# Four fp32r passes for the scores, and values to tokens by block transposes and ScalarE transfers, in a hybrid encoder layer

## The chip, the cores and the metric

The kernel runs on one NeuronCore of one Trainium2 chip, in one launch. The time is the device time of that core in microseconds (us). TensorE (PE in the rows) multiplies, VectorE (DVE), ScalarE (ACT) and GpSimd (POOL) do elementwise work, SyncE (SP) and ScalarE issue the transfers (DMAs).

## The reference

One encoder layer over 512 tokens of 1024 channels, all in float32:

```python
x = x + 0.5 * swiglu(rmsnorm(x, ffn1_norm_g), ...)          # D_FF = 2816
h = rmsnorm(x, mix_norm_g)
aq, ak, av, hq, hff, hfb, hi, hg, ga, gb = split_columns(h @ w_in)
y_attn = axial_gqa_attention(aq, ak, av, q_norm_g, k_norm_g, cos, sin) @ w_branch_attn
y_hgrn = hgrn2_bidirectional(hq, hff, hfb, hi, hg, lb, hgrn_out_norm_g) @ w_branch_hgrn
x = x + (sigmoid(ga) * y_attn + sigmoid(gb) * y_hgrn) @ w_out
x = x + 0.5 * swiglu(rmsnorm(x, ffn2_norm_g), ...)
return rmsnorm(x, final_norm_g)
```

The attention has 8 query heads of 64 channels over 2 key heads. Each head of q and k is normalized (`rmsnorm`), rotated (`apply_rope`), and then `s = q k^T`, `p = softmax(s)`, `o = p v`. In the recurrence (`hgrn2_bidirectional`) `hi` is the value `v`, which is wanted with tokens on the partitions; `hq`, `hff`, `hfb` and `hg` are its query, its two forget gates and its output gate.

## The kernel before, in words

Five engines run programs of their own and meet at semaphores (`wait_ge`, `then_inc`). Each engine takes its instructions in program order, so an instruction that waits holds up all behind it on that engine. The order is written out by hand.

**Weights.** All big products have a "unit" of weights, a tile of 128 x 1024 float32 (512 KB). SyncE loads it into one of two `raw` slots. ScalarE copies it to `w_hi` as fp32r (`split_hi`, L422), VectorE writes the remainder `w_lo = raw - w_hi` (`split_lo`, L791). There are four slots of `w_hi` and `w_lo`, and splits run three units ahead (`AHEAD`). A slot has 1408 columns, of which the units of the projection use the first 1024. TensorE then runs 24 products per unit (8 tiles of 128 channels, each as w_hi*h_hi, w_hi*h_lo, w_lo*h_hi) into one PSUM bank of 128 x 512. With unit `i` finished, VectorE multiplies the bank by the token's norm factor `rs` and puts it into SBUF ("evacuation"; semaphore `proj_read`). Two banks alternate, so unit `i+2` waits for the evacuation of unit `i`.

**The projection.** `PROJ` lists its 26 units: av, ak, four aq, four hi, four hf, four hq, four hf, four hg. All engines loop over it (TensorE L1356, ScalarE L587, VectorE L1000, SyncE L280). Beside the units hang:
- For k and the four q tiles (m = 0 to 4): ScalarE squares, TensorE averages over a head (`head_mean`), ScalarE takes the bias copy, `Ln` and `Exp` at iterations 3 to 7, VectorE a Newton step (three instructions) and the product with the gain (`qn_done`), SyncE swaps halves by four transfers into `q_swap`, GpSimd multiplies by cos, and VectorE finishes the rotation at iterations 4 to 8 (`rope_done`).
- For the values (`V_TILES`: av at iteration 0, hi at iterations 6 to 9): after the evacuation into `v_tmp`, TensorE transposes four 128 x 128 blocks into a PSUM bank (L1371), and ScalarE copies them to `v_a` or `v_h` (L618).
- From iteration 9 (`FIRST_ITEM`) one attention item per unit, 16 in all, `q = i - 9`. After unit `i` TensorE computes the scores of item `q`, 128 queries by 512 keys, for two heads, as plain float32 products over 64 partitions (`scores`, L1321). They wait until ScalarE has taken the exponentials of item `q-1` (`p_done`). VectorE takes the row maxima, ScalarE the exponentials with their sums (`exp_scores`). At the next iteration VectorE inverts the sums, ScalarE normalizes (`normalize_probs`), and VectorE transposes the probabilities by 32 x 32 blocks (`prob_blocks`) ahead of the next maxima.
- SyncE copies `v_a` to `v_rep` by 32 small transfers, ahead of its loads at its iterations 13 to 16 (`V_SENDS`). SyncE's iteration `i` loads unit `i` once `w_lo` of unit `i-2` is written, so it stands some five iterations before VectorE's iteration `i`.

**Order in one ScalarE iteration** from item 0 on: `normalize_probs(q-1)`, `split_hi(i+3)`, the copy of values where there is one, `exp_scores(q)`. **Order in one VectorE iteration:** `inverse_sums(q-1)`, evacuation of unit `i`, `prob_blocks(q-1)` and the maxima of item `q` (`attention_step`), `split_lo(i+3)`.

Elsewhere ScalarE issues transfers as well: in the second FFN, `x_to_tokens` (L443) issues four per call, each of 32 partitions, between its activations.

## Time and profile before

| | us |
|---|---|
| median of 3 runs | 1132.91 |
| lowest, highest | 1132.46, 2531.6 |
| the profiled execution | 1132.66 |
| its span, first to last instruction | 1130.9 |
| TensorE busy, share of the span | 1122.2, 99% |
| VectorE busy | 628.8, 56% |
| ScalarE busy | 442.5, 39% |
| mean granted TensorE clock | 0.998 |

Busy time is that in which an instruction's record covers the engine. Matmul records overlap, since matmuls are pipelined: the record of one 128 x 512 product lasts 389 ns, but the next one starts some 227 ns later. So products are counted here by the distance of their starts. Instructions that issue a transfer are not counted as busy; ScalarE's stand in rows marked ACTq, SyncE's in rows marked SPq. The idle time behind them is put down to "issue".

### The profile page before, as it was taken

The page shows a single profiled execution, that of the slowest core. Times are in us where ns is not written, and L with a number is a line of the kernel's source. Part 1 is how long each engine was busy: PE and PEld are TensorE (multiplying, and loading weights), DVE is VectorE, ACT ScalarE, POOL GpSimd, SP SyncE. Part 2 cuts the span into 40 slices and gives each one's busy share as a digit, 9 for nine tenths or more (in the row PEclk, how much of TensorE's full clock was granted, in tenths as well). Part 3 has the DMA queues.
Part 4 walks back from the last instruction along what each step waited for, and adds up shares of the span by engine and source line. Part 5 has one row for each costly group of instructions (what it writes and reads, how often), then busy time and mean ns, then how long its engine had stood idle before and what let it go on. Part 6 is the DMA issues. An engine that isn't in the chain of part 4 may idle for free.

```text
span 1130.9 us, 16616 instructions
## 1 busy us (share of the span) xinstructions
PE 1122.2 (99%) x6359; PEld 908.6 (80%) x6359; DVE 628.8 (56%) x840; ACT 442.5 (39%) x658; POOL 81.5 (7%) x72
## 2 busy tenths in 40 slices
PE   9999999999999999999999999999999999999997
PEld 7888888888888777777788888888888888888886
DVE  6755555563332586647688767655555555542223
ACT  6423232232222444546856655534232323331223
POOL 0000000000000130000143320020000000000000
PEclk9999999999999999999999999999999999999999
DMA  6332322333322434212221222422244343332321
GB/s 198 124 111 75 111 92 93 108 113 103 103 95 74 172 110 133 75 57 75 76 79 57 74 76 93 168 93 93 79 126 121 91 120 108 119 110 93 99 88 75
DMA packets 51650, 114.78 MB, mean 101 GB/s; under 512 B 21904, under 2 KB 25104, under 8 KB 51344
## 3 DMA queue, kind: packets, MB, share of 16 engines
q1 hardware_dynamic: 32752, 105.16, 28.1%
q10 hardware_dynamic: 18848, 8.92, 2.7%
q8 instruction: 35, 0.57, 0.2%
q14 instruction: 15, 0.12, 0.0%
HBM read 105.41 MB, written 4.19 MB: 97 GB/s over the span
## 4 chain that ended last, share of the span: by engine, by line
PE 98%; DMA 1%; DVE 0%; ACT 0%; ACTq 0%; issue 0%; DVEq 0%
PE ps L1203 27%; PE ps L1205 27%; PE ps L1204 27%; PE ps L1229 4%; PE ps L1228 4%; PE ps L1230 4%; PE ps L1329 1%; PE ps L1346 1%; PE ps L1473 1%; DMA xT<-xT_dram 1%; PE ps L1466 0%; PE ps L1427 0%; PE ps L1449 0%; PE ps L1378 0%; PE ps L1416 0%; DMA raw<-up_dram 0%
## 5 line engine op out<-in xcount | busy, mean ns | idle before, releaser
L1203 PE MATMUL ps<-h_hi,w_hi 128*128 128x512 f32 x1024 | 407.3, 398 | 0.5 <-DVE w_lo L786 0.5
L1205 PE MATMUL ps<-h_hi,w_lo 128*128 128x512 f32 x1024 | 399.1, 390 | 0.0
L1204 PE MATMUL ps<-h_lo,w_hi 128*128 128x512 f32 x1024 | 398.8, 389 | 0.0
L786 DVE TENSOR_TENSOR w_lo<-raw,w_hi 128x1024 fp32r<-128x1024 f32 (+2 forms) x190 | 233.4, 1231 | 176.8 <-ACT w_hi L430 170.6
L430 ACT ACTIVATE w_hi<-raw 128x1024 fp32r<-128x1024 f32 (+1 forms) x182 | 194.7, 1080 | 182.8 <-PE ps L1205 74.3
L1203 PEld LDWEIGHTS ps<-h_hi,w_hi 128*128 128x128 f32 x1024 | 192.2, 188 | 55.8 <-issue 15.2
L1204 PEld LDWEIGHTS ps<-h_lo,w_hi 128*128 128x128 f32 x1024 | 192.3, 188 | 41.7 <-issue 2.9
L1205 PEld LDWEIGHTS ps<-h_hi,w_lo 128*128 128x128 f32 x1024 | 192.2, 188 | 40.6
L502 ACT ACTIVATE g_hi<-un 128x512 fp32r<-128x512 f32 (+1 forms) x44 | 27.8, 632 | 219.9 <-DVE un L786 219.9
L786 DVE TENSOR_TENSOR un<-ps,rs 128x512 f32<-128x512 f32 x44 | 30.4, 690 | 97.6 <-PE ps L1205 97.6
L1229 PE MATMUL ps<-w_hi,g_lo 128*128 128x512 f32 x176 | 68.5, 389 | 0.0
L1205 PE MATMUL ps<-g_hi,w_lo 128*128 128x512 f32 x176 | 68.5, 389 | 0.0
L1203 PE MATMUL ps<-g_hi,w_hi 128*128 128x512 f32 x176 | 68.5, 389 | 0.0
L1228 PE MATMUL ps<-w_hi,g_hi 128*128 128x512 f32 x176 | 68.5, 389 | 0.0
L1230 PE MATMUL ps<-w_lo,g_hi 128*128 128x512 f32 x176 | 68.5, 389 | 0.0
L1204 PE MATMUL ps<-g_lo,w_hi 128*128 128x512 f32 x176 | 68.5, 389 | 0.0
L786 DVE TENSOR_TENSOR g_lo<-un,g_hi 128x512 f32 (+1 forms) x44 | 30.5, 692 | 36.7 <-ACT g_hi L502 36.7
L438 ACT ACTIVATE sq<-xT 128x512 f32 (+1 forms) x16 | 10.1, 632 | 81.0 <-DVE xT L789 81.0
L558 ACT ACTIVATE prob<-ps,neg_max 128x512 f32<-128x512 f32 x32 | 21.7, 685 | 46.5 <-DVE neg_max L974 46.5
L1228 PEld LDWEIGHTS ps<-w_hi,g_hi 128*128 128x128 f32 x176 | 33.0, 188 | 6.9
L1205 PEld LDWEIGHTS ps<-g_hi,w_lo 128*128 128x128 f32 x176 | 33.0, 188 | 6.9
L1204 PEld LDWEIGHTS ps<-g_lo,w_hi 128*128 128x128 f32 x176 | 33.0, 188 | 6.9
(232 smaller groups left out, 1140.6 us busy)
## 6 DMA issues: line engine op xcount, KB each, us to landing
raw<-up_dram SPq DMA_DIRECT2D x86, 512.0 KB, 3.3
raw<-proj_dram SPq DMA_DIRECT2D x26, 512.0 KB, 3.3
raw<-down_dram SPq DMA_DIRECT2D x16, 704.0 KB, 4.0
raw<-down_dram SPq DMA_DIRECT2D x22, 512.0 KB, 3.3
raw<-gates_dram SPq DMA_DIRECT2D x16, 512.0 KB, 3.3
raw<-branch_dram SPq DMA_DIRECT2D x8, 512.0 KB, 3.3
raw<-wout_dram SPq DMA_DIRECT2D x8, 512.0 KB, 3.3
x_spill_dram<-xT ACTq DMA_DIRECT2D x1, 2048.0 KB, 7.1
```

Of the source, the lines that this page charges most:

```text
L430: A(w_hi[:, cst % 4, 0:width], raw[:, cst % 2, 0:width], ACT.Copy).then_inc(hi_done, 1)
L502: A(g_hi[:, 2 * it + q, :], un[:], ACT.Copy).then_inc(ghi_done, 1)
L558: A(prob[:, a, :], ps[:, 2 + a, :], ACT.Exp, bias=neg_max[:, q, a:a + 1], accum_out=prob_sum[:, q, a:a + 1]).then_inc(p_done, 1)
L786: return V.tensor_tensor(out, a, b, op)
L1203: T.matmul(ps[:, bank, :], w_hi[:, slot, cols], moving_hi(j), start=start and j == 0, stop=False)
L1204: T.matmul(ps[:, bank, :], w_hi[:, slot, cols], moving_lo(j), start=False, stop=False)
L1205: ins = T.matmul(ps[:, bank, :], w_lo[:, slot, cols], moving_hi(j), start=False, stop=stop and j == tiles - 1)
L1228: T.matmul(ps[:, bank, :], g_hi[:, j, rows], w_hi[:, slot, cols], start=first, stop=False)
L1229: T.matmul(ps[:, bank, :], g_lo[:, j, rows], w_hi[:, slot, cols], start=False, stop=False)
L1230: ins = T.matmul(ps[:, bank, :], g_hi[:, j, rows], w_lo[:, slot, cols], start=False, stop=end)
L1329: T.matmul(ps[:, 2 + a, :], qk[rows, 1 + t, P * qt:P * (qt + 1)], qk[rows, 0, :], start=True, stop=True).then_inc(s_done, 1)
L1346: ins = T.matmul(ps[rows, Y_BANK + i, GROUP * BLOCK * w:GROUP * BLOCK * (w + 1)], v_rep[j // 8][keys, j % 8, rows], probs.rearrange("p s c ...
```

## The change

**Scores.** The two float32 products of an item over 64 partitions become four fp32r products over 128 partitions. The keys are split into a high part, held twice (`k_twice`, both halves of the partitions), and a low part (`k_low`, also on both halves), in the free columns of the `w_hi` and `w_lo` slots. The queries of a head are split into `q_parts`: high part on one half of the partitions, low part on the other. ScalarE writes the high parts (`keys_twice` at iteration 6, four copies; `query_hi` at 7, 10, 13, 17, two copies each) and the second half of the low keys (`keys_low_swapped` at 9, two copies); VectorE writes the low parts (`keys_low` at 8, `query_low` at 8, 11, 14, 18, two instructions each).

**Splits ahead of norms.** At iterations 3 to 7 the splits of the weights stand ahead of the norm's instructions on both engines, and the Newton step's square moves from VectorE to ScalarE.

**Values to tokens.** hi moves behind the first four hf, to iterations 10 to 13. TensorE's transposes of hi and ScalarE's copies to `v_h` go. Instead VectorE transposes `v_tmp` in place by 32 x 32 blocks right after the evacuation, and ScalarE, after `exp_scores`, issues 16 transfers of 32 partitions x 4 x 32 elements (16 KB) that put the blocks in place in `v_h` (`values_to_tokens`). The next hi's evacuation on VectorE waits until all 16 have landed (`vh_loaded`), because they read `v_tmp`.

**Smaller things.** SyncE's first `v_rep` transfer also waits for `rope_done` 5. The sigmoids also wait for the last scores.

```diff
--- before.py
+++ after.py
@@ -61,11 +61,15 @@
 
 
 
-PROJ = ([("av", 0), ("ak", 0)] + [("aq", t) for t in range(4)] + [("hi", t) for t in range(4)]
-        + [("hf", h) for h in range(4)] + [("hq", t) for t in range(4)]
+PROJ = ([("av", 0), ("ak", 0)] + [("aq", t) for t in range(4)] + [("hf", h) for h in range(4)]
+        + [("hi", t) for t in range(4)] + [("hq", t) for t in range(4)]
         + [("hf", h) for h in range(4, HH)] + [("hg", t) for t in range(4)])
-V_TILES = {i: w for w, i in enumerate(i for i, (kind, _) in enumerate(PROJ) if kind in ("av", "hi"))}
+V_TILES = {0: 0}
+HI_AT = PROJ.index(("hi", 0))
 FIRST_ITEM = 9
+KEYS_AT = [6, 9]
+QUERY_AT = [7, FIRST_ITEM + 1, FIRST_ITEM + 4, FIRST_ITEM + 8]
+LOW_AT = [8, FIRST_ITEM + 2, FIRST_ITEM + 5, FIRST_ITEM + 9]
 BLOCK = 32
 BLOCKS = S // BLOCK
 QUADS = P // BLOCK
@@ -169,8 +173,13 @@
         q_cos = prob
         q_swap = [at("q_swap0", 16, [P, S]), at("q_swap1", 18, [P, S])]
         v_tmp = at("v_tmp", 85, [P, S])
+        q_parts = [at("q_parts0", 32, [P, 2, S], F32R)] + [at(f"q_parts{n}", kib, [P, 2, S], F32R) for n, kib in ((1, 87), (2, 91))]
+        q_parts.append(q_parts[1])
+        k_twice = [w_hi[:, 2 * a:2 * a + 2, UW:UW + S // 2] for a in range(2)]
+        k_low = [w_lo[:, 2 * a:2 * a + 2, UW:UW + S // 2] for a in range(2)]
         q_sq, q_ms, q_rs, q_t = (at(n, 87 + 2 * i, [P, S]) for i, n in enumerate(("q_sq", "q_ms", "q_rs", "q_t")))
         silu_tmp = [q_sq, q_ms, q_rs, q_t]
+        q_t = [q_t, at("q_t1", 82, [P, S])]
 
         k_in = [at("k_in0", 64, [P, S]), sq_sum]
         b_cum = [at("b_cum0", 66, [P, S]), at("b_cum1", 68, [P, S])]
...
@@ -290,6 +302,7 @@
                             to = i - V_SENDS
                             if to == 0:
                                 sp.wait_ge(vn_done, 1)
+                                sp.wait_ge(rope_done, 5)
                             for half in range(2):
                                 for quad in range(QUADS):
                                     sp.dma_start(v_rep[half][BLOCK * to:BLOCK * (to + 1), quad::QUADS, :],
@@ -550,6 +563,38 @@
                     split_hi(2)
             ffn(1)
 
+            halves = lambda k: k.rearrange("p (s c) -> p s c", s=2)
+
+            def keys_twice():
+                act.wait_ge(rope_done, 1)
+                for a, rows in enumerate(head_rows):
+                    for to in (rows, head_rows[1 - a]):
+                        A(k_twice[a][to], halves(qk[rows, 0, :]), ACT.Copy).then_inc(khi_done, 1)
+
+            def keys_low_swapped():
+                act.wait_ge(klo_done, 2)
+                for a, rows in enumerate(head_rows):
+                    A(k_low[a][head_rows[1 - a]], k_low[a][rows].bitcast(F32), ACT.Copy).then_inc(kls_done, 1)
+
+            def query_hi(t):
+                act.wait_ge(rope_done, t + 2)
+                if t == 0:
+                    act.wait_ge(qsq_done, 1)
+                elif t < 3:
+                    act.wait_ge(rope_done, 5)
+                else:
+                    act.wait_ge(s_done, 16)
+                for a, rows in enumerate(head_rows):
+                    A(q_parts[t][rows, a, :], qk[rows, 1 + t, :], ACT.Copy).then_inc(qhi_done, 1)
+
+            def values_to_tokens(w):
+                act.wait_ge(vblk_done, w + 1)
+                blocks = v_tmp[:].rearrange("p (t j c) -> p t j c", j=QUADS, c=BLOCK)
+                for quad in range(QUADS):
+                    for to in range(QUADS):
+                        act.dma_start(v_h[BLOCK * to:BLOCK * (to + 1), :, P * w + BLOCK * quad:P * w + BLOCK * (quad + 1)],
+                                      blocks[BLOCK * quad:BLOCK * (quad + 1), :, to, :]).then_inc(vh_loaded, 16)
+
             def exp_scores(q):
                 for a in range(2):
                     act.wait_ge(nm_done, 2 * q + 1 + a)
@@ -571,6 +616,7 @@
             def sigmoids():
 
                 act.wait_ge(proj_read, len(PROJ) + BANK_CREDIT)
+                act.wait_ge(s_done, 2 * ITEMS)
                 for j in range(HH):
                     A(forget[:, j, :], forget[:, j, :], ACT.Sigmoid).then_inc(fs_done, 1)
                     if j >= 4:
@@ -590,6 +636,7 @@
                     act.wait_ge(lb_ready, 1)
                     A(lbt[:], lbt[:], ACT.Exp).then_inc(lb_exp, 1)
                 if 3 <= i <= 7:
+                    split_hi(base + i + AHEAD)
                     m = i - 3
                     act.wait_ge(qms_done, m + 1)
                     if m:
@@ -599,9 +646,17 @@
                     A(q_rs[:], q_ms[:], ACT.Ln).then_inc(act_seq, 1)
                     act.wait_ge(act_seq, m + 1)
                     A(q_rs[:], q_rs[:], ACT.Exp, scale=-0.5).then_inc(qr_done, 1)
+                    act.wait_ge(qr_done, m + 1)
+                    if m >= 2:
+                        act.wait_ge(rope_done, m - 1)
+                    A(q_t[m % 2][:], q_rs[:], ACT.Square).then_inc(qy_done, 1)
+                if i in KEYS_AT:
+                    (keys_twice, keys_low_swapped)[KEYS_AT.index(i)]()
+                if i in QUERY_AT:
+                    query_hi(QUERY_AT.index(i))
                 if 0 <= i - FIRST_ITEM - 1 < ITEMS:
                     normalize_probs(i - FIRST_ITEM - 1)
-                for n in {0: (0, 1), 1: ()}.get(i, (i,)):
+                for n in {0: (0, 1), 1: ()}.get(i, () if 3 <= i <= 7 else (i,)):
                     split_hi(base + n + AHEAD)
                 if i == 0:
                     rms_estimate(1)
@@ -615,13 +670,15 @@
                 if w is not None:
                     act.wait_ge(vt_done, w + 1)
                     vt = ps[:, 7, :].rearrange("p (a b) -> p a b", b=P)
-                    A(v_a[:] if w == 0 else v_h[:, :, P * (w - 1):P * w], vt, ACT.Copy).then_inc(vn_done, 1)
+                    A(v_a[:], vt, ACT.Copy).then_inc(vn_done, 1)
                 q = i - FIRST_ITEM
                 if q == Y_AT:
                     y_hi(0)
                     y_hi(1)
                 if 0 <= q < ITEMS:
                     exp_scores(q)
+                if kind == "hi":
+                    values_to_tokens(t)
             gate_base = BASE["gates"]
 
 
@@ -947,6 +1004,19 @@
                 tt(by_quad(ya_lo[:, t, :]), ps[:, Y_BANK:Y_BANK + QUADS, P * t:P * (t + 1)].rearrange("p i (s c) -> p s i c", c=BLOCK),
                    by_quad(ya_hi[:, t, :].bitcast(F32)), ALU.subtract).then_inc(yalo_done, 1)
 
+            halves = lambda k: k.rearrange("p (s c) -> p s c", s=2)
+
+            def keys_low():
+                dve.wait_ge(khi_done, 4)
+                for a, rows in enumerate(head_rows):
+                    tt(k_low[a][rows], halves(qk[rows, 0, :]), k_twice[a][rows].bitcast(F32), ALU.subtract).then_inc(klo_done, 1)
+
+            def query_low(t):
+                dve.wait_ge(qhi_done, 2 * t + 2)
+                for a, rows in enumerate(head_rows):
+                    tt(q_parts[t][head_rows[1 - a], a, :], qk[rows, 1 + t, :], q_parts[t][rows, a, :].bitcast(F32),
+                       ALU.subtract).then_inc(qlo_done, 1)
+
             def inverse_sums(q):
                 dve.wait_ge(p_done, 2 * q + 2)
                 V.reciprocal(inv_sum[:, q, :], prob_sum[:, q, :]).then_inc(inv_done, 1)
@@ -1001,15 +1071,17 @@
                 if i == 2:
                     lower_bound()
                 if 3 <= i <= 7:
+                    split_lo(base + i + AHEAD)
                     m = i - 3
-                    dve.wait_ge(qr_done, m + 1)
-                    link(newton(q_rs[:], q_ms[:], q_t[:]))
+                    dve.wait_ge(qy_done, m + 1)
+                    link(stt(q_t[m % 2][:], q_t[m % 2][:], -0.5, q_ms[:], ALU.mult, ALU.mult))
+                    link(stt(q_rs[:], q_t[m % 2][:], 1.5, q_rs[:], ALU.add, ALU.mult))
                     stt(qk[:, m, :], qk[:, m, :], gain[:, 33:34] if m == 0 else gq8[:], q_rs[:],
                         ALU.mult, ALU.mult).then_inc(qn_done, 1)
                     dve.wait_ge(qn_done, m + 1)
                 if 0 <= i - FIRST_ITEM - 1 < ITEMS:
                     inverse_sums(i - FIRST_ITEM - 1)
-                if i != 1 and i < FIRST_ITEM:
+                if i != 1 and i < FIRST_ITEM and not 3 <= i <= 7:
                     split_lo(base + i + AHEAD)
                 if i == 0:
                     split_lo(base + 1 + AHEAD)
@@ -1017,24 +1089,32 @@
                 if i - FIRST_ITEM == Y_AT:
                     y_lo(0)
                     y_lo(1)
-                w = V_TILES.get(i)
-                if w:
-                    dve.wait_ge(vt_done, w)
+                if kind == "hi":
+                    dve.wait_ge(*((vh_loaded, 16 * QUADS * QUADS * t) if t else (vt_done, 1)))
                 dst = {"av": v_tmp[:], "hi": v_tmp[:], "ak": qk[:, 0, :], "aq": qk[:, min(1 + t, 4), :], "hf": forget[:, t, :],
                        "hq": hq[:, t % 4, :], "hg": hgate[:, t % 4, :]}[kind]
                 dve.wait_ge(unit_done, base + i + 1 + W_CREDIT)
                 tt(dst, ps[:, i % 2, :], rs[:], ALU.mult).then_inc(proj_read, 1)
+                if i == LOW_AT[0]:
+                    keys_low()
                 if 4 <= i <= 8:
                     m = i - 4
                     dve.wait_ge(mix_loaded, 16)
                     dve.wait_ge(qswap_done[m % 2], 64 * (m // 2 + 1))
-                    link(tt(q_t[:], q_swap[m % 2][:], c["sin"], ALU.mult))
+                    link(tt(q_t[m % 2][:], q_swap[m % 2][:], c["sin"], ALU.mult))
                     dve.wait_ge(cos_done, m + 1)
-                    tt(qk[:, m, :], q_cos[:, m % 2, :], q_t[:], ALU.add).then_inc(rope_done, 1)
+                    tt(qk[:, m, :], q_cos[:, m % 2, :], q_t[m % 2][:], ALU.add).then_inc(rope_done, 1)
                     dve.wait_ge(rope_done, m + 1)
+                if i == LOW_AT[0]:
+                    query_low(0)
+                if kind == "hi":
+                    dve.wait_ge(proj_read, i + 1 + BANK_CREDIT)
+                    V.transpose(v_tmp[:], v_tmp[:]).then_inc(vblk_done, 1)
                 attention_step(i - FIRST_ITEM)
                 if i >= FIRST_ITEM:
                     split_lo(base + i + AHEAD)
+                if i in LOW_AT[1:]:
+                    query_low(LOW_AT.index(i))
             gate_base = BASE["gates"]
 
             def gate_lo(g):
@@ -1321,19 +1401,22 @@
             def scores(q):
                 t, qt = q // 4, q % 4
                 if q == 0:
-                    pe.wait_ge(rope_done, 5)
+                    pe.wait_ge(khi_done, 4)
+                    pe.wait_ge(kls_done, 2)
+                if qt == 0:
+                    pe.wait_ge(qlo_done, 2 * t + 2)
                 for a in range(2):
                     if q:
                         pe.wait_ge(p_done, 2 * q - 1 + a)
-                    rows = slice(HD * a, HD * (a + 1))
-                    T.matmul(ps[:, 2 + a, :], qk[rows, 1 + t, P * qt:P * (qt + 1)], qk[rows, 0, :],
-                             start=True, stop=True).then_inc(s_done, 1)
+                    queries = q_parts[t][:, a, P * qt:P * (qt + 1)]
+                    T.matmul(ps[:, 2 + a, :], queries, k_twice[a], start=True, stop=False)
+                    T.matmul(ps[:, 2 + a, :], queries, k_low[a], start=False, stop=True).then_inc(s_done, 1)
 
             def weighted(w):
                 if w == 0:
                     pe.wait_ge(vrep_loaded, 16 * 2 * QUADS * QUADS)
                     pe.wait_ge(qeps_done, 5)
-                    pe.wait_ge(vn_done, 5)
+                    pe.wait_ge(vn_done, 1)
                 else:
                     pe.wait_ge(yalo_done, 2 * w)
                 pe.wait_ge(pt_done, TURNS * GROUP * (w + 1))
@@ -1439,7 +1522,7 @@
             def contributions(u):
                 pe.wait_ge(kn_done, u + 1)
                 if u == 0:
-                    pe.wait_ge(vn_done, 5)
+                    pe.wait_ge(vh_loaded, 16 * QUADS * QUADS * 4)
                 if u >= 3:
                     pe.wait_ge(oeps_done, (u - 1) // 2)
                 for n in range(NSUP):
```

## Rows read from the trace of the kernel before

**Rows 1.** The page: busy time of each engine, and the chain that ended last by engine.
```profile
PE 1122.2 (99%) x6359; PEld 908.6 (80%) x6359; DVE 628.8 (56%) x840; ACT 442.5 (39%) x658; POOL 81.5 (7%) x72
PE 98%; DMA 1%; DVE 0%; ACT 0%; ACTq 0%; issue 0%; DVEq 0%
```

**Rows 2.** TensorE's longest wait in the whole span: us in total, times, longest.
```profile
PE ps L1315 <- POOL g_lo L316: 1.3, 1, 1.3
```

**Rows 3.** The chain in order of time: start us, us, what (L1371 transposes, L1329 scores).
```profile
417.71 0.44 PE ps L1371 x4
...
423.64 0.44 PE ps L1371 x4
...
443.97 1.06 PE ps L1329 x4
...
450.71 1.06 PE ps L1329 x4
...
851.90 0.23 PE ps L1204
...
862.78 0.23 PE ps L1204
```

**Rows 4.** ScalarE in order of time, second FFN: start, length, what, idle before it.
```profile
823.94 2.59 ACTq L448 DMA_DIRECT2D x_tok<-xT  x4
826.63 2.01 ACT L430 ACTIVATE w_hi<-raw 128x1024 fp32r<-128x1024 f32 x2 [2.07 <-issue]
```

**Rows 5.** Busy us by stretch, before item 0: PE, PEld, DVE, ACT, POOL, PEclk, DMA, GB/s.
```profile
372.00:430.00 58.00, 57.90 (x253) 45.34 (x251) 42.66 (x60) 26.40 (x38) 11.61 (x5) 1.00 0.41 139
```

**Rows 6.** VectorE in order of time, iteration 10 (item 1).
```profile
436.80 0.69 DVE L786 TENSOR_TENSOR forget<-ps,rs 128x512 f32<-128x512 f32 x1 [3.20 <-PE ps L1205]
437.41 0.70 DVE L962 STREAM_TRANSPOSE prob_t<-prob 128x512 f32<-128x512 f32 x1
438.04 0.85 DVE L965 STREAM_TRANSPOSE prob_t<-prob 128x128 f32<-128x128 f32 x4
438.81 1.25 DVE L974 TENSOR_REDUCE neg_max<-ps 128x1 f32<-128x512 f32 x2
```

**Rows 7.** SyncE in order of time, and VectorE's last rotation, before item 0.
```profile
424.15 6.71 SPq L295 DMA_DIRECT2D v_rep<-v_a  x8
...
427.66 0.69 DVE L786 TENSOR_TENSOR qk<-prob,q_t 128x512 f32<-128x512 f32 x1
```

**Rows 8.** Instructions that issue transfers, by tile: ns min/median/max; below, time to landing.
```profile
L448 ACTq DMA_DIRECT2D x_tok<-xT x64: 592/632/744, 815.0 to 976.2; - x64
...
L295 SPq DMA_DIRECT2D v_rep<-v_a x32: 585/597/1778, 424.2 to 447.5; - x32
...
L298 SPq DMA_DIRECT2D raw<-proj_dram x26: 327/328/586, 333.7 to 516.2; - x26
...
DMA to landing us min/median/max: 1.8/1.9/3.9
```

**Rows 9.** ScalarE in order of time, item 1.
```profile
439.49 0.69 ACT L558 ACTIVATE prob<-ps,neg_max 128x512 f32<-128x512 f32 x1 [1.66 <-DVE neg_max L974]
...
440.74 0.20 ACT L558 ACTIVATION_READ_ACCUMULATOR prob<-ps,neg_max 128x1 f32 x1
441.30 1.34 ACT L564 ACTIVATE prob<-prob,inv_sum 128x512 f32<-128x512 f32 x2 [0.36 <-DVE inv_sum L952]
```

**Rows 10.** The end of the span, by stretches: TensorE busy first, PEclk after POOL.
```profile
1124.00:1126.00 2.00, 0.35 (x2) 0.00 (x0) 1.66 (x5) 1.57 (x4) 0.00 (x0) 1.00 0.38 145
1126.00:1128.00 2.00, 0.00 (x0) 0.00 (x0) 1.21 (x4) 1.09 (x3) 0.00 (x0) 0.67 0.59 228
1128.00:1130.90 2.90, 0.00 (x0) 0.00 (x0) 0.00 (x0) 0.00 (x0) 0.00 (x0) 0.50 0.47 181
```

**Rows 11.** TensorE in order of time, the start of the span.
```profile
1.32 5.06 PE L1315 MATMUL ps<-g_lo 128*128 128x512 f32 x11 [1.32 <-POOL g_lo L316]
...
8.41 0.61 PE L1263 MATMUL ps<-h_hi,w_hi 128*128 128x512 f32 x2
```

More of the change, by code:

```diff
@@ L215, in build @@
         vt_done, vn_done = sem("vt_done"), sem("vn_done")
+        vblk_done, vh_loaded = sem("vblk_done"), sem("vh_loaded")
         qsq_done, qms_done, qeps_done, qr_done = sem("qsq_done"), sem("qms_done"), sem("qeps_done"), sem("qr_done")
-        cos_done = sem("cos_done")
+        cos_done, qy_done = sem("cos_done"), sem("qy_done")
+        khi_done, klo_done, kls_done = sem("khi_done"), sem("klo_done"), sem("kls_done")
+        qhi_done, qlo_done = sem("qhi_done"), sem("qlo_done")
         qn_done, rope_done = sem("qn_done"), sem("rope_done")
```

## The prediction

> **What bounds the kernel now.** I read the page first: TensorE is busy for 99% of the span and the chain of waits that ended last runs on it for 98% [rows 1]. Then TensorE's waits: the longest is 1.3 us, at the very start [rows 2]. So in this kernel every TensorE product taken away is time saved, and every wait of TensorE that appears is time lost; nothing else counts. Then the chain in order of time, for what one step costs TensorE. A unit with nothing beside it takes (862.78 - 851.90) / 2 = 5.44 us (48 products, two units), a unit with a transpose of values 423.64 - 417.71 = 5.93, a unit with a score item 450.71 - 443.97 = 6.74 [rows 3]. Last I read what ScalarE pays for issuing a transfer, because the change gives it 64 more: four take 2.59 us, and the split behind them begins only when they are through, with 2.07 us of idle time put down to "issue" [rows 4]. ScalarE does not work while it issues.
>
> **What the change takes from TensorE.** Scores: an item costs 6.74 - 5.44 = 1.30 us now. Four fp32r products of 128 x 512 at the pace of a unit's (5.44 / 24 = 0.227 us) are 0.91. Saved: 16 x 0.39 = 6.2 us. No row has products with these operands; the bounds are 0.91 (same engine, same size, same kind) and 1.30 (nothing gained), and I take the first, since the new products have the form of a unit's. Transposes: 4 x (5.93 - 5.44) = 2.0 us. Together **8.2 us less**, if nothing waits.
>
> **The stretch before item 0.** At iterations 3 to 7 VectorE loses a square of 0.7 us per round and ScalarE gains it, which is busy for 26.4 of the 58 us of this stretch [rows 5]; the new copies of keys and queries (eight of some 0.6 us before item 0) fit beside it. The tight place is VectorE at iteration 8. With TensorE's transposes gone, unit 8 ends at 417.7 + 5.44 = 423.1 (start of the first removed transpose plus a unit) and unit 9 at 428.6. From 423.1 on VectorE does evacuation, `keys_low` (2), the two instructions of the rotation and `query_low` (2), seven instructions of 0.6 to 0.7 us [rows 6]: done at about 427.8. Item 0 is then ready 0.8 us before TensorE wants it. I cost this at nothing, bounds 0 and 2 us. The rotation ends near 426.5, where it ended at 428.3 before, but SyncE now holds the first eight `v_rep` transfers until then, where they began at 424.15 [rows 7]; they take 6.7 us at most, so raw 13, behind them on that queue, is issued near 433 and has landed by 437 (3.9 at most [rows 8]), so that ScalarE can split it ahead of item 1's exponentials at 438. Nothing, again because of cover: the loss is 0 to 2 us if that cover is gone.
>
> **The four hi iterations.** Here I see the loss. ScalarE issues 16 transfers behind the exponentials of each of items 1 to 4. At 2.59 / 4 = 0.645 us each [rows 4] that is **10.3 us in which ScalarE stands still**, in an iteration that TensorE wants to do in 5.44 + 0.91 = 6.35. Behind them on ScalarE wait the next normalization, the next split and the next exponentials, and TensorE's scores of item q wait for the exponentials of item q-1. Besides, VectorE waits for the landing before it evacuates the next hi, and behind that evacuation stand the block transposes and the maxima which those same exponentials need. One turn of this ring, from end of exponentials to end of exponentials:
> - 15 issues of 0.645, then 1.9 from the last issue to landing [rows 8]: 11.6 us; 0.1 for the signal.
> - VectorE: evacuation 0.61 (start to start), the new transpose 0.63 and a wait of 0.1 for the write before it, `prob_blocks` 438.81 - 437.41 = 1.40 [rows 6]; then from first maximum to first exponential 0.68 and the exponentials 440.94 - 439.49 = 1.45 [rows 6, 9]. Sum 4.9.
>
> A turn is 16.6 us against 6.35. The fourth train delays no evacuation, since iteration 14 is hq; there the ring is 10.3 of issue, then 1.34 of normalization, 0.8 for the last block transposes, and 0.68 + 1.45: 14.6 us.
>
> Now the clock times. Unit 9 ends at 428.6, unit 10 at 428.6 + 6.35 = 434.95, and the exponentials of item 1 end at 434.95 + 4.9 = 439.8. The next three ends are 456.4, 473.0, 489.6, and after the fourth train 504.2. The first head's exponential, which releases TensorE, is 0.65 earlier each time. TensorE wants item 2's scores at 441.3 (nothing to wait for) and item 3's at 447.65:
> - item 3: 455.8 instead of 447.65, waits 8.1 us
> - items 4 and 5: each a turn later, less unit and scores (5.44 + 1.1, since the second head now waits for its own exponential): 16.6 - 6.5 = 10.1 us each
> - item 6: 14.6 - 6.5 = 8.1 us
>
> With the 0.2 us per item that makes **37.1 us**. After item 6 ScalarE has no train any more and the ring (about 6.3 us) fits into the unit again. What is late next: nothing, the splits of units 16 and 17 are written inside the last two waits.
>
> **The clock.** The waits of 8 to 10 us are long enough to lose TensorE's clock. The last product of this kernel ends at 1124.35; the granted clock is 1.00 up to 1126, 0.67 in the next two microseconds and 0.50 after [rows 10]: it fell from 2.4 to 1.2 GHz between 2 and 3 us after the work stopped. What a return costs is seen at the start: 11 products take 5.06 us, 0.46 each, twice 0.227, and at 8.41 two take 0.61 together, the full pace [rows 11]. So some 6 us of work go at half pace, a loss of 3 us. Inside the ring this is free (unit and scores of 6.5 us become 9.5, the turn is 16.6); only after the fourth wait is it on the path. I take **3 us**; bounds 0 and 3.
>
> The Trainium skill, page "TensorE: Matmul & The Clock Gate", section "HAM oscillation — how this bites in real kernels", says that a kernel which waits between groups of products falls back to the lower level and pays the return at each such wait. By that rule there would be four returns to pay; the end of this trace agrees on the fall, no row shows how often the return is paid.
>
> **Sum.** 1132.66 (the profiled execution; 0.25 below the median, the span is 1130.9) - 8.2 + 37.1 + 3.0 = **1164.6, say 1165 us**, 2.8% slower.
>
> **Rivals.**
> - *Issuing is cheap.* SyncE's loads of 128 partitions take 0.33 us to issue, not 0.6 [rows 8]. If the new transfers did, with 128 pieces each instead of x_tok's 256: a turn is 11.9 us, the waits 3.4, 5.3, 5.3 and 3.6, with the 0.2s about 18; 1132.7 - 8.2 + 18 + 1 = 1143. Against it: `v_rep`, with 32 partitions and only 64 pieces, takes 0.597 [rows 8], so the number of pieces is not what costs. Chance 0.13.
> - *Issuing is hidden altogether* (not slower): the instructions only pass into a queue and ScalarE goes on, the landing of 2 us fits into the unit, and only TensorE's saving is left: 1132.66 - 8.2 = 1124.5. It holds if ScalarE's next activation begins within about 2 us of a train's start. Against it the idle time of 2.07 us behind four issues [rows 4]. Chance 0.07.
> - *Trains cost more.* No row has 16 issues in a row from ScalarE. The slowest x_tok issue took 0.744, landing took up to 3.9 and one `v_rep` issue 1.78 where loads stood on the same queue [rows 8]. In the first train SyncE issues `v_rep` at the same time. At 0.744 and with 3.9 to land three times: 37 + 6.3 + 6 = 49 us, 1177. Chance 0.12.
> - *Each return is paid.* If unit and scores at half pace came to stand in the ring after all (the second head's scores wait inside it), four returns of 3 us cost 12 instead of 3: 1174. Against it: a turn leaves 7 us after such a unit. The Trainium skill's section on HAM oscillation is on this side. Chance 0.02.
> - *The passes save nothing*, or item 0 stalls: 2 to 6 us on top of the forecast, 1167 to 1171. Chance 0.05, on top of any of the others; within the range.
>
> The Trainium skill, page "DMA: Bandwidth & Descriptors", section "Issuing engines are not separate DMA queues", says that the sequencer's time to start a transfer is usually small against the transfer. By it the second rival would hold and the time be 1124.5; here four issues occupy 2.59 us and one transfer lands in 1.9, so the trace disagrees, and the rival gets 0.07.
>
> **How the numbers follow.** Forecast 0.66 (1155 to 1172: issues of 0.585 to 0.70, the clock's 0 to 3 us), dearer trains 0.12 (to 1180), four returns 0.02, cheap issues 0.13 (1143, up to 1155), hidden 0.07 (1124). The range 1145 to 1180 leaves out the last, half of the cheap case and a little above: under 2 in 10. What a measurement can tell from no change is about 2%, here 23 us, so 1156 upward is slower: the forecast but for its lowest edge, the dear case and the four returns, 0.78. Within 2%: 0.21. Faster by 2% would need 22.7 us off TensorE, and 8.2 is all that is taken away: 0.01.
>
> **What would show it.** In the changed kernel's TensorE waits, four that end with ScalarE's exponentials, of about 8, 10, 10 and 8 us, between 447 and 504, and nothing of size elsewhere. In ScalarE's order of time, four trains of 16 issues, 10 us each, with no activation inside. On VectorE three waits for landings of about 10 us. The granted clock at 0.5 in part of that stretch. Score items outside it with 6.35 us from unit to unit. I am wrong if activations begin during a train, if the issues take 0.33, or if TensorE's gap per item stays at 6.74.

## The result, and the profile after

| | before | changed |
|---|---|---|
| median, us | 1132.92 (4 runs) | 1164.14 (4 runs, 1163.08 to 1164.68) |
| span of the profiled execution | 1130.9 | 1161.3 |
| mean granted clock | 0.998 | 0.986 |

The ratio is 1.0277, 95% interval 1.0263 to 1.0291: **slower by 2.8%**, 31.2 us. The forecast was 1165. (One run of the kernel before took 2531.6 us; the comparison leaves it out.)

The page of the changed kernel, against [rows 1]: TensorE's busy time hardly moves and its share falls, so most of the added time is time without work (the idle time grows from 8.7 to 36.9 us). The chain now runs for 3% of the span through ScalarE's issuing instructions.

```profile
PE 1124.4 (97%) x6343; PEld 920.4 (79%) x6343; DVE 635.9 (55%) x849; ACT 451.7 (39%) x673; POOL 76.4 (7%) x72
PE 87%; DVE 5%; ACTq 3%; ACT 2%; DMA 1%; issue 1%; DVEq 0%
```

TensorE's waits in the changed kernel (total, times, longest), against [rows 2]: five for the exponentials (L603; four are of size, the fifth is 0.6 us at item 11), the one at the very start, and one for the low part of the queries.

```profile
PE ps L1412 <- ACT prob L603: 27.6, 5, 7.4
PE ps L1395 <- POOL g_lo L329: 1.3, 1, 1.3
PE ps L1412 <- DVE q_parts L843: 0.7, 1, 0.7
```

TensorE in order of time in the changed kernel, the first of an item's four passes, items 2 to 8:

```profile
441.86 0.39 PE L1412 MATMUL ps<-w_hi,q_parts 128*128 128x512 f32 x1
...
455.81 0.80 PE L1412 MATMUL ps<-w_hi,q_parts 128*128 128x512 f32 x1 [7.44 <-ACT prob L603]
...
471.54 0.77 PE L1412 MATMUL ps<-w_hi,q_parts 128*128 128x512 f32 x1 [6.89 <-ACT prob L603]
...
487.90 0.80 PE L1412 MATMUL ps<-w_hi,q_parts 128*128 128x512 f32 x1 [6.96 <-ACT prob L603]
...
501.80 0.79 PE L1412 MATMUL ps<-w_hi,q_parts 128*128 128x512 f32 x1 [5.70 <-ACT prob L603]
...
509.71 0.39 PE L1412 MATMUL ps<-w_hi,q_parts 128*128 128x512 f32 x1
...
516.05 0.39 PE L1412 MATMUL ps<-w_hi,q_parts 128*128 128x512 f32 x1
```

Where nothing disturbs, an item and its unit take 516.05 - 509.71 = 6.34 us, where they took 6.74 [rows 3]. The four intervals before are 13.95, 15.73, 16.36 and 13.90 long, together 34.6 us more than 4 x 6.34. The idle times in brackets add up to 27.0 only, because after each wait the products ran at half pace (0.43 from start to start instead of 0.23) and filled a part of the next interval. Read the loss from starts, not from idle times.

ScalarE in order of time in the changed kernel, around the second train, items 2 and 3:

```profile
454.98 0.69 ACT L603 ACTIVATE prob<-ps,neg_max 128x512 f32<-128x512 f32 x1 [2.34 <-DVE neg_max L1044]
455.56 0.19 ACT L603 ACTIVATION_READ_ACCUMULATOR prob<-ps,neg_max 128x1 f32 x1
455.58 0.59 ACTq L595 DMA_DIRECT2D v_h<-v_tmp  x1
455.66 0.68 ACT L603 ACTIVATE prob<-ps,neg_max 128x512 f32<-128x512 f32 x1
456.21 0.62 ACTq L595 DMA_DIRECT2D v_h<-v_tmp  x1
456.23 0.20 ACT L603 ACTIVATION_READ_ACCUMULATOR prob<-ps,neg_max 128x1 f32 x1
456.86 9.10 ACTq L595 DMA_DIRECT2D v_h<-v_tmp  x14
466.01 1.33 ACT L609 ACTIVATE prob<-prob,inv_sum 128x512 f32<-128x512 f32 x2 [9.58 <-issue]
467.25 1.04 ACT L443 ACTIVATE w_hi<-raw 128x1024 fp32r<-128x1024 f32 x1
470.62 0.69 ACT L603 ACTIVATE prob<-ps,neg_max 128x512 f32<-128x512 f32 x1 [2.33 <-DVE neg_max L1044]
```

The train is there, 10.4 us for 16 issues (0.65 each), and nothing behind it begins before it is over. Its first two issues, though, lie beside the second exponential, which begins at 455.66, 0.08 us after the first issue.

VectorE's waits in the changed kernel from 440 to 500 us (total, times, longest): three for the landing, and one for the normalization behind the fourth train.

```profile
DVE v_tmp L843 <- DMA v_h<-v_tmp: 30.8, 3, 11.3
DVE prob_t L1032 <- ACT prob L609: 9.4, 1, 9.4
```

The stretches of the changed kernel around the first wait (busy us of PE first, the granted clock after POOL's), against [rows 10]:

```profile
448.00:450.00 2.00, 0.37 (x2) 0.00 (x0) 0.00 (x0) 0.00 (x0) 0.00 (x0) 1.00 0.51 108
450.00:452.00 2.00, 0.00 (x0) 0.00 (x0) 0.43 (x1) 1.65 (x3) 0.00 (x0) 1.00 0.29 65
452.00:454.00 2.00, 0.00 (x0) 0.00 (x0) 1.97 (x6) 0.63 (x1) 0.00 (x0) 0.91 0.00 0
454.00:456.00 2.00, 0.19 (x1) 0.19 (x2) 2.00 (x6) 1.02 (x3) 0.00 (x0) 0.50 0.00 0
456.00:458.00 2.00, 2.00 (x5) 1.57 (x6) 1.94 (x3) 0.42 (x2) 0.00 (x0) 0.50 0.27 39
458.00:460.00 2.00, 2.00 (x6) 1.52 (x6) 0.27 (x2) 0.00 (x0) 0.00 (x0) 0.50 0.79 263
460.00:462.00 2.00, 2.00 (x10) 1.59 (x9) 0.00 (x0) 0.00 (x0) 0.00 (x0) 0.88 0.16 26
```

The engine stopped at 448.4, the clock went from 2.4 to 1.2 GHz between 452 and 454, and came back soon after 460, some 4.5 us after the work had begun again at 455.8.

The fourth wait, in windows of 1 us. TensorE had stopped at 496.1:

```profile
501.00:502.00 1.00, 0.20 (x1) 0.20 (x2) 1.00 (x2) 1.00 (x3) 0.00 (x0) 0.72 0.00 0
...
504.00:505.00 1.00, 1.00 (x4) 0.75 (x4) 0.85 (x3) 0.67 (x2) 0.00 (x0) 0.58 0.95 373
```

A mean of 0.72 over this microsecond puts the fall near 501.4, only 0.4 us before the work began again at 501.80; a mean of 0.58 puts the rise near 504.8.

### The profile page after: what moved, and what is told of

Read it like the earlier page. It is cut to its first block, busy times and chain, and to the rows that moved or that the text cites. A ratio compares the mean times of both kernels' runs of the same rounds, so it can differ in the third digit from the quotient of the medians.

```text
span 1161.3 us, 16682 instructions
## 1 busy us (share of the span) xinstructions
PE 1124.4 (97%) x6343; PEld 920.4 (79%) x6343; DVE 635.9 (55%) x849; ACT 451.7 (39%) x673; POOL 76.4 (7%) x72
## 4 chain that ended last, share of the span: by engine, by line
PE 87%; DVE 5%; ACTq 3%; ACT 2%; DMA 1%; issue 1%; DVEq 0%
PE ps L1283 24%; PE ps L1284 24%; PE ps L1285 24%; PE ps L1310 3%; PE ps L1309 3%; PE ps L1308 3%; ACTq L595 3%; PE ps L1429 1%; PE ps L1556 1%; DVE w_lo L843 1%; ACT w_hi L443 1%; DMA v_h<-v_tmp 0%; PE ps L1412 0%; DMA xT<-xT_dram 0%; DVE prob_t L1035 0%
## 5 line engine op out<-in xcount | busy, mean ns | idle before, releaser
L843 DVE TENSOR_TENSOR un<-ps,rs 128x512 f32<-128x512 f32 x44 | 30.4, 690 | 98.1 <-PE ps L1285 98.1
L1412 PE MATMUL ps<-w_hi,q_parts 128*128 128x512 f32 x32 | 15.4, 482 | 28.3 <-ACT prob L603 27.6
L1309 PEld LDWEIGHTS ps<-w_hi,g_lo 128*128 128x128 f32 x176 | 33.0, 188 | 6.9
```

The lines of the kernel that those rows point to most:

```text
L843: return V.tensor_tensor(out, a, b, op)
L1309: T.matmul(ps[:, bank, :], g_lo[:, j, rows], w_hi[:, slot, cols], start=False, stop=False)
L1412: T.matmul(ps[:, 2 + a, :], queries, k_twice[a], start=True, stop=False)
```

## The experiments

The experiments ran on three chips, with the kernel before beside them: at 1132.16 us for the parts, the own tiles and SyncE's version, at 1132.22 for the spread issues, all fillers and the trimmed version, at 1132.46 for the last filler, the repetition and the undone splits.

**One part alone: the scores without the transfers.** The values' path is that of before (hi stays behind the first hf):

```diff
-V_TILES = {0: 0}
+V_TILES = {i: w for w, i in enumerate(i for i, (kind, _) in enumerate(PROJ) if kind in ("av", "hi"))}
...
-                if kind == "hi":
-                    values_to_tokens(t)
...
-                if kind == "hi":
-                    dve.wait_ge(*((vh_loaded, 16 * QUADS * QUADS * t) if t else (vt_done, 1)))
+                w = V_TILES.get(i)
+                if w:
+                    dve.wait_ge(vt_done, w)
...
-                    V.transpose(v_tmp[:], v_tmp[:]).then_inc(vblk_done, 1)
```

> The changed kernel with the values' path put back: TensorE transposes hi and ScalarE copies it to v_h, no block transposes, no transfers (hi stays behind the first hf). Theory (ScalarE stands still while it issues, all of the loss is in the four trains): the four waits of TensorE go, the score items keep 6.35 us from unit to unit, and 16 x 0.40 = 6.4 us are saved less about 1.5 us of waits at items 0 and 10; 1126.5 to 1129 us. Rival (the stretch with splits, keys and queries on VectorE and ScalarE is what stalls): stays above 1150 us.

Measured: 1128.41 us, ratio 0.9967 (0.9955 to 0.9979). Inside the range; the rival is out. Scores, splits, keys and queries are a gain of 3.7 us by themselves.

**The other part alone: the transfers with the scores of before.** The kernel before, with hi moved, the block transposes and the transfers:

```diff
+            def values_to_tokens(w):
...
+                if kind == "hi":
+                    values_to_tokens(t)
```

> The kernel before with only the values' path of the change: hi behind the first hf, block transposes, 64 transfers by ScalarE; float32 scores over 64 partitions and the norms as before. Theory: four waits of TensorE of about 7 us each, ended by the exponentials, since the turns of 15.8, 15.7, 16.4 and 13.9 us are set by ScalarE and VectorE, and an item of 6.74 us instead of 6.35 only fills a little more of them: 1132.9 - 2.0 (transposes) + 33 + 1.5 (clock) = 1165 us, between 1161 and 1168. Rival (scores and transfers disturb each other): well under 1150 us.

Measured: 1166.69 us, ratio 1.0304 (1.0288 to 1.0320). TensorE's waits in this kernel:

```profile
PE ps L1342 <- ACT prob L567: 23.4, 4, 6.9
```

Four waits, and a loss of 34.5 us. The values' path is the whole cause of the loss. The two parts nearly add up: 34.5 - 3.7 = 30.8, and the change measured 31.2. The expectation was 1.7 us short; a term of it that was too small is the clock's (1.5). TensorE at items 6 and 7:

```profile
500.82 2.74 PE L1342 MATMUL ps<-qk 64*128 64x512 f32 x4 [3.64 <-ACT prob L567]
...
510.89 1.13 PE L1342 MATMUL ps<-qk 64*128 64x512 f32 x4
```

The step behind the fourth wait took 10.07 us against 6.74, 3.3 more. Here the clock stood at 1.2 GHz for the first 6.3 us of it, where it did so for 3.0 us in the changed kernel.

**Which half of the ring: landing or issuing.** The block transposes go to tiles of their own, so that the next evacuation waits for no landing. ScalarE issues as in the change. (The tiles lie where later work writes, so behind the projection ScalarE also waits for the last landing.)

```diff
+        v_blk = [at(f"v_blk{n}", kib, [P, S]) for n, kib in enumerate((20, 22, 28, 30))]
...
-                    dve.wait_ge(*((vh_loaded, 16 * QUADS * QUADS * t) if t else (vt_done, 1)))
+                    dve.wait_ge(*((vblk_done, t) if t else (vt_done, 1)))
...
-                    V.transpose(v_tmp[:], v_tmp[:]).then_inc(vblk_done, 1)
+                    V.transpose(v_blk[t][:], v_tmp[:]).then_inc(vblk_done, 1)
```

> The changed kernel, but the block transposes write into four tiles of their own, so VectorE evacuates the next hi without waiting for the landing; ScalarE issues the same 16 transfers behind the exponentials. Theory (the issue time on ScalarE is the larger part of the ring, landing and evacuation the smaller): every turn becomes like the fourth one, 13.9 us, so the first three lose 1.9, 1.8 and 2.5: 6 us less than the changed kernel, 1158 us. Rival (the wait for the landing is the cause, issuing alone would be hidden): all four waits vanish, 1126 us.

Measured: 1160.71 us, ratio 1.0255 (1.0240 to 1.0271). The rival is out: with no wait for a landing left the kernel is still 28.5 us slower than before. The gain (2.7 us in the spans, 1161.3 to 1158.6; 3.4 in the medians) is less than the 6 expected. ScalarE's order of time in this kernel, the first head's exponentials of items 1 to 5:

```profile
438.91 0.69 ACT L604 ACTIVATE prob<-ps,neg_max 128x512 f32<-128x512 f32 x1 [1.50 <-DVE neg_max L1046]
...
452.96 0.69 ACT L604 ACTIVATE prob<-ps,neg_max 128x512 f32<-128x512 f32 x1 [0.58 <-DVE neg_max L1046]
...
466.86 0.69 ACT L604 ACTIVATE prob<-ps,neg_max 128x512 f32<-128x512 f32 x1 [0.58 <-DVE neg_max L1046]
...
482.96 0.69 ACT L604 ACTIVATE prob<-ps,neg_max 128x512 f32<-128x512 f32 x1 [0.58 <-DVE neg_max L1046]
...
496.85 0.69 ACT L604 ACTIVATE prob<-ps,neg_max 128x512 f32<-128x512 f32 x1 [0.58 <-DVE neg_max L1046]
```

The turns are 14.05, 13.90, 16.10 and 13.89 us. The third has the copies of queries (1.3 us), which in the changed kernel lay beside the landing and now stand in the ring, and an issue of 1.46. So I had mis-sized the third turn: taking one wait away puts what it covered on the path. The turns are 3.8 us shorter in sum. Of that 0.6 went to the clock: the step behind the fourth wait took 8.51 us here, 7.91 in the changed kernel.

**Another queue issues.** With the same own tiles, SyncE issues the 64 transfers, eight ahead of each of its loads 18 to 25.

```diff
+                        if 18 <= i < 26:
+                            w = (i - 18) // 2
+                            sp.wait_ge(vblk_done, w + 1)
...
+                            for quad in (2 * (i % 2), 2 * (i % 2) + 1):
+                                for to in range(QUADS):
+                                    sp.dma_start(v_h[BLOCK * to:BLOCK * (to + 1), :, P * w + BLOCK * quad:P * w + BLOCK * (quad + 1)],
```

> The changed kernel with four tiles of their own for the transposed blocks, and SyncE issues the 64 transfers, eight ahead of each of its loads 18 to 25 (5.1 us of issue plus a load against a unit of 6.35 us). Theory: ScalarE is free again, no wait for exponentials in hi's iterations, TensorE keeps both savings: 1132.9 - 8.2 + about 1.5 of small waits (items 0 and 10) = 1126 us, and faster than both kernels by 0.5%. Rival (the transfers themselves load the DMA engines so that weights come late, or SyncE's queue becomes the bound): TensorE waits for splits, 1130 us or more.

Measured: 1126.97 us, ratio 0.9953 (0.9939 to 0.9966). The same 64 transfers, off ScalarE, cost little: against the scores alone (1128.41) this kernel has the transposes' 2.0 us less on TensorE and is 1.4 faster, which leaves some 0.6. So moving the data was not the cause. This edit changes two things at once, the issuing engine and the size of a train (eight instead of sixteen); the next pair keeps ScalarE and changes the size alone. The waits left, 0.7 at item 0 and 0.6 at item 11:

```profile
PE ps L1420 <- DVE q_parts L851: 0.7, 1, 0.7
PE ps L1420 <- ACT prob L612: 0.6, 1, 0.6
```

**Spread over 16 iterations.** ScalarE issues again, from own tiles, four per iteration: behind the exponentials in the first kernel, ahead of them in the second.

```diff
-                if kind == "hi":
-                    values_to_tokens(t)
+                if i >= HI_AT:
+                    values_to_tokens((i - HI_AT) // QUADS, [(i - HI_AT) % QUADS])
```

> As e3 (own tiles for the transposed blocks, ScalarE issues), but the 64 issues are spread: four per iteration over iterations 10 to 25, behind the exponentials, where normalization's wait of 0.36 us for the inverse is hidden by them. Theory (an issue is 0.65 us of ScalarE's time, wherever it stands): the turn of 13.9 us with 16 issues leaves 3.5 us without; with four it is 6.1, just inside TensorE's 6.35, and about 7.4 in the two iterations in which two copies of queries stand in it. So 1127 plus 1 to 2 us: 1127 to 1130 us. Rival (what costs is the number of transfers in total, 64 small ones by ScalarE, 0.65 x 64 = 42 us of it): stays above 1150 us.

> As e6_four_behind, but the four issues stand between the split and the exponentials (one iteration later), where ScalarE was idle for 2.65 us before the change. Theory: ScalarE's work in an iteration is 1.45 + 0.36 (waiting for the inverse) + 1.24 + 0.95 + 2.6 = 6.6 us, more than TensorE's 6.35, so each of 16 iterations loses about 0.25: 1131 us. Rival (any place in which ScalarE is idle hides them): 1127 us, not above e6_four_behind.

Measured: 1128.30 us behind them, ratio 0.9965 (0.9951 to 0.9979), and 1127.67 ahead of them, ratio 0.9961 (0.9946 to 0.9976). So 64 issues by ScalarE, four at a time, cost about 1 us more than SyncE's version (1.4 and 0.9 by the ratios), which refutes the first rival: the cause is a train of sixteen behind the last activation of the ring. The runs of the first kernel spread from 1127.21 to 1130.78 us, so the two places are not to be ranked by their medians. But for the second kernel my theory was wrong and its rival right. ScalarE in order of time there:

```profile
459.73 0.72 ACT L610 ACTIVATE prob<-prob,inv_sum 128x512 f32<-128x512 f32 x1 [0.36 <-DVE inv_sum L1025]
459.83 0.59 ACTq L596 DMA_DIRECT2D v_h<-v_blk  x1
460.36 0.71 ACT L610 ACTIVATE prob<-prob,inv_sum 128x512 f32<-128x512 f32 x1
460.45 0.62 ACTq L596 DMA_DIRECT2D v_h<-v_blk  x1
460.98 1.04 ACT L444 ACTIVATE w_hi<-raw 128x1024 fp32r<-128x1024 f32 x1
461.10 1.28 ACTq L596 DMA_DIRECT2D v_h<-v_blk  x2
463.49 0.69 ACT L604 ACTIVATE prob<-ps,neg_max 128x512 f32<-128x512 f32 x1 [1.47 <-DVE neg_max L1047]
```

The normalization and the split stand ahead of the four issues in the program and still run while they are issued: the first issue begins at 459.83, before the second normalization (460.36) and the split (460.98). I read this as ScalarE having handed over those activations, which wait for nothing more, before it came to the issues. The 2.6 us of issue lie beside 2.2 us of activations. So "ScalarE stands still while it issues", as I had put it, holds only for what is **behind** the issues.

**The clock.** TensorE runs 24 extra products into an unused bank ahead of items 3 to 6 (first kernel) or of item 6 alone (second kernel), so that it stands still for less time.

```diff
+                if 3 <= q <= 6:
+                    for _ in range(24):
+                        T.matmul(ps[:, 7, :], k_twice[0][:, 0, 0:P], h_hi[:, 0, :], start=True, stop=True)
```

> The changed kernel, but TensorE runs 24 extra products of 128 x 512 into an unused bank ahead of the scores of items 3, 4, 5 and 6 (5.4 us each at 2.4 GHz, less than each wait). Theory: the granted clock stays at 1.00, the waits still end with the exponentials at the same time, and only the half-pace work behind the fourth wait is gone: scores and unit 16 took 7.9 us where they take 6.35, so 1.5 us less than the changed kernel, 1162.5 us. If all four returns were on the path, 4 to 6 us less, 1159 us. If the fall of the clock had no part in it: 1164 us.

> The changed kernel with 24 extra products ahead of the scores of item 6 alone, so that only the fourth wait is filled. In e7_fillers the last return of the clock was gone (6.7 us from the start of item 6's scores to item 7's, instead of 7.9) but the median did not move, and two issues in its trains took 1.65 and 1.83 us where the changed kernel had one of 1.39. Theory A (the clock's return costs 1.2 to 1.5 us on the path; fillers in the first three waits moved the trains against SyncE's loads and lost as much again): 1.2 us less than the unchanged e11_after_again. Theory B (the return costs nothing in the end, because the exponentials of item 6 set the pace behind the fourth wait too): equal to e11_after_again within 0.4 us.

> The changed kernel as it is, on the same chip as e10_filler_last and e8_norms_first, for a comparison of 1 us: 1163.5 us here, since the kernel before runs at 1132.2 on the chips of the other experiments.

Measured: 1163.55 us with all fillers, ratio 1.0277 (1.0263 to 1.0291), the very ratio of the changed kernel; 1161.59 with the last alone, ratio 1.0257 (1.0243 to 1.0271); the unchanged kernel beside it 1164.52, ratio 1.0287 (1.0273 to 1.0301). TensorE with the last filler alone, the first pass of items 6 and 7:

```profile
501.92 0.50 PE L1415 MATMUL ps<-w_hi,q_parts 128*128 128x512 f32 x1
...
508.62 0.39 PE L1415 MATMUL ps<-w_hi,q_parts 128*128 128x512 f32 x1
```

This step is 6.70 us where the unchanged one took 8.14 in the same group (502.21 to 510.35) and 7.91 in the first profile. The fourth return of the clock therefore costs 1.2 to 1.4 us on the path by these traces; the medians say 2.9, with intervals that leave room for 0.2 to 6.6. Theory A holds for the last filler. Fillers in the first three waits bring nothing. They did not all keep the clock either. In the second wait TensorE still stood idle for 4.39 us behind its fillers, and the clock fell, against my expectation that it stays at 1.00 (PEclk after POOL):

```profile
470.00:472.00 2.00, 0.00 (x0) 0.00 (x0) 2.00 (x7) 0.21 (x1) 0.00 (x0) 0.87 0.00 0
472.00:474.00 2.00, 1.38 (x3) 1.12 (x4) 1.56 (x3) 1.24 (x4) 0.00 (x0) 0.50 0.05 8
```

Besides, the turns of that kernel are 15.8, 16.7, 15.7 and 15.1 us, 1.5 in sum more than in the changed kernel, with issues of 1.65 and 1.83 us in two trains. Why the issues grew in that kernel was not settled.

**The splits ahead of norms.** The SyncE version with this part of the change undone: splits behind the norms, the square on VectorE.

```diff
-                    split_lo(base + i + AHEAD)
...
-                    link(stt(q_t[m % 2][:], q_t[m % 2][:], -0.5, q_ms[:], ALU.mult, ALU.mult))
-                    link(stt(q_rs[:], q_t[m % 2][:], 1.5, q_rs[:], ALU.add, ALU.mult))
+                    link(newton(q_rs[:], q_ms[:], q_t[m % 2][:]))
```

> e4_sync_issues with one part of the change undone: the splits stand behind the norms again and the Newton square is on VectorE (five instructions of 0.7 us more there). Theory (VectorE is the tight engine before item 0: it is busy without a break from 412 to 429.6, and item 0 waits 0.7 us for it): item 0 waits 3 us or more, and 1129 to 1131 us against 1127.0. Rival (the part makes no difference, TensorE is fed from slots split three units ahead): 1127 us.

Measured: 1128.63 us, ratio 0.9971 (0.9959 to 0.9983). Its TensorE waits for the low queries:

```profile
PE ps L1415 <- DVE q_parts L848: 2.2, 1, 2.2
```

2.2 us instead of 0.7, and the median 1.7 above the 1126.97 of SyncE's version. The direction is as expected, the size (3 us) was too large, and the median lies below the expected 1129 to 1131. The two ran on different chips and their intervals overlap, so the firmer evidence is the wait, which VectorE ends: this part of the change, its two halves together, is worth some 1.5 us.

**A version that beats both.** The SyncE version, and two instructions' places changed: the split of unit 11 behind the low queries of item 0, and the last low queries two iterations later.

```diff
-LOW_AT = [8, FIRST_ITEM + 2, FIRST_ITEM + 5, FIRST_ITEM + 9]
+LOW_AT = [8, FIRST_ITEM + 2, FIRST_ITEM + 5, FIRST_ITEM + 11]
...
-                if i != 1 and i < FIRST_ITEM and not 3 <= i <= 7:
+                if i != 1 and i < FIRST_ITEM and not 3 <= i <= 8:
...
                 if i == LOW_AT[0]:
                     query_low(0)
+                    split_lo(base + i + AHEAD)
```

> e4_sync_issues with the two small waits of the change taken away: VectorE's split of unit 11 goes behind query_low(0) (item 0 waited 0.7 us for it), and query_low(3) goes from iteration 18 to 20 (it stood ahead of the exponentials for which item 10 waited 0.6 us and more). Theory: 1 to 2 us less than e4: 1125 to 1126 us. Rival (other work on VectorE becomes late instead): no change, 1127 us.

Measured: 1125.01 us, ratio 0.9937 (0.9923 to 0.9950), **faster than the kernel before by 7.2 us** and than the changed one by about 39. That is 0.6%, small but clear of the interval. Neither of the two waits is among TensorE's any more. At the scores of item 15 the kernel is 8.3 us ahead of the kernel before (530.32 against 538.60), the saving on TensorE that was forecast as 8.2; about 1 us of it is lost again in the recurrence, and no run says why.

## Why the prediction was right

Point by point, with the profiled execution's numbers:

- *What is taken from TensorE*: 8.2 us forecast. An item takes 6.34, so 16 x 0.40 = 6.4, and with the 2.0 of the transposes 8.4. The trimmed version, without the ring, is 8.3 ahead at item 15 and 7.2 at the end. Right.
- *The stretch before item 0*: costed at nothing, 0 to 2. It was 0.7, the wait for the low queries. VectorE took unit 8 up at 424.03 and not at its end near 423, since the split of unit 11 stood ahead of it, which my count from 423.1 had left out.
- *The ring*: turns of 16.6, 16.6, 16.6 and 14.6 were forecast, 15.8, 15.6, 16.5 and 13.9 came (454.98 - 439.19 and so on). The mechanism is the forecast one, engine by engine. The term that was mis-sized is the train's start: I let it begin behind both exponentials, and the first one or two issues ran beside the second, some 0.8 us each turn. The third turn lost that again, to an issue of 1.39. The delay to item 6's scores came to 34.6 us, where the sum has 37.1 (the forecast's own clock times give 503.55 - 466.7 = 36.9). Taken by the letter, one of the signs of being wrong was seen, since the second exponential begins inside each train, some 0.08 us after its first issue. Behind the third issue no activation starts until the train is over.
- *The clock*: 3 forecast, bounds 0 and 3; 7.91 - 6.34 = 1.6 in the changed kernel, 1.2 to 1.4 by the filler. It rose after 3 us of work there, not after 6. The size is this kernel's alone: the same step lost 2.2 us with the own tiles (8.51) and 3.3 with the transfers alone (10.07), so returns of about 3 do occur, and rows 10 and 11 could not tell how long the half pace would last here. (In rows 11 the half pace was read from the distance of the products; the granted clock stands at 1.00 there.) That only the fourth return is on the path was right: the first three lie inside the turns, as the starts above show. The Trainium skill, page "TensorE: Matmul & The Clock Gate", section "HAM oscillation — how this bites in real kernels", has every such wait fall back and pay; the trace agrees that the clock falls in all four (near 453.6, 467.3, 484.4 and 501.4), and disagrees that each is paid in time.
- *Not in the forecast*: the last low queries, at iteration 18, delay the exponentials once more, and items 10 to 12 lose 1.3 us (starts at 529.58, 536.08, 543.21, 549.90 against steps of 6.34). With these moved, in the trimmed version, 1.1 of the 1.3 is gone (492.04 to 511.23 for the same three steps). The prediction costs the new copies and low parts before item 0 alone. Those of iterations 10 to 18 stand in no term; up to iteration 14 none of TensorE's waits ends with them, at iteration 18 one does.
- Sum: -8.4 + 34.6 + 1.6 + 0.7 + 1.3 = 29.8, against 30.4 in the spans. The 0.6 between them stands in no term. The profiled execution took 1163.08, 1.5 less than my sum of 1164.6: a ring 2.5 us and a clock 1.4 us too dear, against 2.0 of small waits that I had at nothing and the 0.6. That the total came so close is in part luck, since these errors cancel; the ring alone was 2.5 off in 34.6.

The rivals: *issuing is cheap* fell to the trains (0.65 each from start to start, 0.59 at best). *Issuing is hidden* fell to the 9.6 to 10.4 us of "issue" idle behind every train, but with four issues ahead of the exponentials it turned out true where something already handed over can run beside the issues. The Trainium skill, page "DMA: Bandwidth & Descriptors", section "Issuing engines are not separate DMA queues", calls the initiating time usually small against the transfer; here an issue takes 0.62 us against 1.9 to landing, a third of it, and the 16 add up to 10.4, so for small transfers in a train the trace disagrees. *Dearer trains* came in part: one issue of 1.39 in this kernel, up to 1.83 in the variants.

## What to carry to other kernels

Count each issued transfer of this kind as 0.65 us of the issuing engine's program, and ask what stands behind it. In front of a wait that is there anyway it was free; behind the last activation of a ring all but the first one or two were on the path. When an edit saves a few us on an engine that is busy for 99%, ask first whether it makes that engine wait: lay out one turn of the ring that the edit closes (who issues, who waits for the landing, who waits for that one) before counting the saving. A buffer that transfers read should not be the one that the next evacuation needs; here that alone was worth 2.7 to 3.4 us.

## What the runs showed of the hardware that I had not expected

- Issuing instructions and activations overlap in one direction: four issues (2.6 us) ran beside the normalization and split that stood ahead of them.
- A single issue in a train can take two to three times the usual: 1.39, 1.52 and 1.65 us. Each of these began 0.81 us after SyncE had issued a 512 KB load (472.34 and 473.15 in the changed kernel, 472.58 and 473.39 in its repetition, 456.81 and 457.62 with fillers). But this distance comes from the order of the ring: in the changed kernel's second train an issue began 0.81 us after a load as well (456.70 and 457.51) and took 0.62. Others were long at another distance, 1.83 us (489.18 and 491.94) and, with the last filler alone, 1.32 us (472.54 and 472.69). The cause stays open.
- The granted clock fell 5.3, 2.7, 3.4 and 5.3 us after TensorE stopped in the four waits of the changed kernel (at 448.4, 464.6, 480.9 and 496.1), and 2 to 3 us after the last product of the kernel before [rows 10]. It rose some 4.7, 6.0, 3.3 and 3.0 us after work began again (at 455.8, 471.5, 487.9 and 501.8). So one and the same kernel pays a different price at each return, and the price can be read only where the return is on the path.
